# The decay differences of a chunked linear attention, issued on VectorE instead of GpSimd

## The reference

```python
def chunked_gated_linear_attention(q, k, v, log_g):
    '''S_t = diag(g_t) S_{t-1} + k_t^T v_t ; o_t = q_t S_t, evaluated chunkwise.'''
    ...
# ab_layer: GLA_HEADS = 4, key size 128, value size 256
ob = chunked_gated_linear_attention((qb * GLA_DK ** -0.5), kb, vb, log_a)
# cd_layer: HGRN_HEADS = 8, key and value size 128
od = chunked_gated_linear_attention(silu(qd), 1.0 - f, idd, log(f))
```

## Time and profile before

| | |
|---|---|
| median of 3 runs | 3214.06 us (3213.27 to 3218.4) |
| the profiled execution | 3213.27 us, of which the profile's span is 3212.0 us |
| TensorE busy | 3055.3 us (95%) |
| VectorE busy | 2129.2 us (66%) |
| ScalarE busy | 1527.7 us (48%) |
| GpSimd busy | 164.7 us (5%) |

### The profile page before, as it was taken

How to read it: one execution, slowest core, us unless ns; L and a number is a source line. 1 busy time by engine, 2 the same in 40 slices (tenths; PEclk the granted TensorE clock), 3 DMA queues, 4 the chain that set the end, 5 groups by cost and what they waited for, 6 DMA issues and landing times. The chain is left out here.

```text
span 3212.0 us, 57240 instructions
## 1 busy us (share of the span) xinstructions
PE 3055.3 (95%) x25845; PEld 2600.1 (81%) x25870; DVE 2129.2 (66%) x2024; ACT 1527.7 (48%) x1406; POOL 164.7 (5%) x292
## 2 busy tenths in 40 slices
PE   8999899999999999999999999998999899789896
PEld 7888788888888787587888888887686787657785
DVE  5555766666556666458687786555665547898785
ACT  4343654445434544745555555334554534333652
POOL 0000000000000000001200000000400000002220
PEclk9999999999999999999999999999999999899998
DMA  8665456655656454445766666563545445554331
GB/s 287 208 205 191 139 203 210 209 197 195 225 185 210 149 172 167 169 158 166 260 236 213 228 230 216 205 202 115 171 157 188 167 171 186 171 184 168 119 135 62
DMA packets 295477, 596.75 MB, mean 186 GB/s; under 512 B 11825, under 2 KB 16049, under 8 KB 295105
## 3 DMA queue, kind: packets, MB, share of 16 engines
q1 hardware_dynamic: 287616, 564.22, 51.4%
q0 software_dynamic: 7616, 28.87, 2.4%
HBM read 577.32 MB, written 15.73 MB: 185 GB/s over the span
## 5 line engine op out<-in xcount | busy, mean ns | idle before, releaser
L1489 DVE TENSOR_TENSOR WL<-WF,WH 128x2048 bf16<-128x2048 f32 x533 | 1208.5, 2288 | 682.3 <-ACT WH L999 682.1
L531 PE MATMUL PSG<-XH,WH 128*128 128x256 bf16 x5648 | 1549.9, 274 | 52.4 <-DVE XL L1594 26.3
L531 PE MATMUL PSG<-XL,WH 128*128 128x256 bf16 x5648 | 1549.7, 274 | 0.0
L531 PE MATMUL PSG<-XH,WL 128*128 128x256 bf16 x5648 | 1548.8, 274 | 0.0
L999 ACT ACTIVATE WH<-WF 128x2048 bf16<-128x2048 f32 x533 | 999.9, 1899 | 615.4 <-PE PSG L531 372.2
L531 PE MATMUL PSG<-SCR,WH 128*128 128x256 bf16 x4480 | 736.8, 273 | 0.0
L531 PEld LDWEIGHTS PSG<-XH,WH 128*128 128x128 bf16 x5648 | 556.4, 99 | 134.7 <-issue 65.5
L531 PEld LDWEIGHTS PSG<-XL,WH 128*128 128x128 bf16 x5648 | 555.9, 98 | 69.9 <-issue 1.2
L531 PEld LDWEIGHTS PSG<-XH,WL 128*128 128x128 bf16 x5648 | 556.1, 98 | 67.8
L531 PE MATMUL PSG<-SCR,WL 128*128 128x256 bf16 x2240 | 610.6, 273 | 0.0
L531 PEld LDWEIGHTS PSG<-SCR,WH 128*128 128x128 bf16 x4480 | 438.5, 98 | 55.0
(11 more groups left out here) (240 smaller groups left out, 1652.5 us busy)
## 6 DMA issues: line engine op xcount, KB each, us to landing
WF<-ffn_w_up SPq DMA_DIRECT2D x176, 1024.0 KB, 5.8
WF<-ffn_w_down SPq DMA_DIRECT2D x88, 1024.0 KB, 5.1
WF<-ab_w_in SPq DMA_DIRECT2D x56, 1024.0 KB, 5.2
WF<-a_w_in SPq DMA_DIRECT2D x48, 1024.0 KB, 6.0
WF<-cd_w_in SPq DMA_DIRECT2D x48, 1024.0 KB, 5.2
WF<-a_w_out SPq DMA_DIRECT2D x16, 1024.0 KB, 5.1
WF<-kv_w_k SPq DMA_DIRECT2D x16, 1024.0 KB, 5.1
WF<-b_w_q SPq DMA_DIRECT2D x16, 1024.0 KB, 5.1
```

The source lines that it names most:

```text
L531: return nc.tensor.matmul(o, lhsT, rhs, start=start, stop=stop, skip_group_check=True)
L1489: tt(l, w, h, ALU.subtract).then_inc(s_lo, 1)
```

## The change

The 15 instructions per head go from GpSimd's stream to VectorE's. The first 14 are the same operations with the same operands; the last becomes a tensor_scalar with b's column 127 as the pointer operand. decay(0) and decay(1) take the first two side steps of VectorE's flow, ahead of weigh(0), which were empty; decay(h+2) takes step 5 of head h, right after the step with weigh(h+1), which was empty too. ScalarE's and TensorE's streams stay as they are. GpSimd has no compute left in these stretches; its DMA issues stay in their order.

```diff
         def gpsimd_program():
-            def decays(P):
-                for h in range(P["H"]):
-                    n, bb, e = P["base"] + h, P["b"][:, h, :], P["E"][h % 2]
-                    if h >= 2:
-                        nc.gpsimd.wait_ge(s_prod, 2 * n - 2)
-                    for l in range(1, 8):
...
-                        nc.gpsimd.tensor_tensor(to[:, :, 0:half], mid, src[:, :, 0:half], ALU.subtract)
-                        nc.gpsimd.tensor_tensor(to[:, :, half:width], src[:, :, half:width], mid, ALU.subtract)
-                    last = bb[:, 127:128].broadcast_to([128, 128])
-                    nc.gpsimd.tensor_tensor(e[:, 7, 0:128], last, bb[:, 0:128], ALU.subtract).then_inc(s_dec, 1)
...
-            nc.gpsimd.wait_ge(s_scan, 1)
-            decays(GLA)
...
-            nc.gpsimd.wait_ge(s_scan, 2)
-            nc.gpsimd.wait_ge(s_xs, 16)
-            nc.gpsimd.wait_ge(s_yb, 16)
-            decays(HGRN)
...
             def gla_heads(P):
+                def decay(h):
+                    n, bb, e = base + h, P["b"][:, h, :], E[h % 2]
+                    if h >= 2:
+                        nc.vector.wait_ge(s_prod, 2 * n - 2)
+                    for l in range(1, 8):
+                        width = 2 ** l
+                        half = width // 2
+                        src = bb.rearrange("p (n w) -> p n w", w=width)
+                        to = e[:, l - 1, :].rearrange("p (n w) -> p n w", w=width)
+                        mid = src[:, :, half - 1:half].broadcast_to([128, T // width, half])
+                        tt(to[:, :, 0:half], mid, src[:, :, 0:half], ALU.subtract)
+                        tt(to[:, :, half:width], src[:, :, half:width], mid, ALU.subtract)
+                    ts(e[:, 7, 0:128], bb[:, 0:128], bb[:, 127:128], -1.0, ALU.subtract, ALU.mult).then_inc(s_dec, 1)
...
                     if h + 1 < H:
                         weigh(h + 1)
                     yield
+                    if h + 2 < H:
+                        decay(h + 2)
                     yield
                     yield
                     yield
...
-                yield
+                decay(0)
+                yield
+                decay(1)
                 yield
                 weigh(0)
```

## The result

The changed kernel takes 3240.1 us (median of 4 runs, 3235.8 to 3245.9) against 3214.2 us before (4 runs, 3213.3 to 3218.4). The ratio is 1.0075, its 95% interval 1.0055 to 1.0095. The forecast was 3239 us. The profiled execution of the changed kernel took 3238.2 us with a span of 3236.9 us. That is 24.9 us more span than before (3212.0).

The account below looks back on a forecast made before the run. TensorE, busy 95% of the span, bounds GLA; HGRN has about 30 us of TensorE holes. GLA 8.6 + HGRN 18 = 26.6 us, taken as 26 on 3213.3, gives 3239 us; own range 3233 to 3246, wider range 3222 to 3252.

Parts of the forecast that it names:

- The rates: VectorE: decay 0.207 us an instruction, 3.1 us a head; 37 us of work added, 13 regained from weigh, net 24.
- GLA, forecast 8.6: GLA stretch: 4.4 + 1.5 + 1.1 + 1.6 = 8.6 us, all staying because TensorE is full there.
- The start: GLA start: TensorE stands 4.4 us as decay(0) delays weigh(0), then 1.5 us more at the lower clock.
- the steps after it: GLA heads 0 and 1: later exponentials delay TensorE's norm by 1.1 us, then 1.6 more in the next head.
- HGRN, forecast 18: HGRN stretch: delays at the start and heads 0 to 5, 18 us; heads 6 and 7 have no decay.
- forecast step: HGRN norms: start +0.3, head 0 +2.4, then +6.3, +2.0, +3.1, +1.0 and +2.9 us for heads 1 to 5.
- not only work, it is also queued: VectorE: decay also waits behind mask, sum, scaling, weigh and often a split, so ScalarE waits longer at exponentials.
- Throughput alone: Rival: only net VectorE work on the chain counts, 11 us in HGRN, 4.4 at GLA's start; 3229 us, 27%.
- No change: Rival: VectorE's slack and the lead of three chunks cover each shift, TensorE sees nothing; 3213 us, 6%.
- Stalls that slow the clock: Rival: each of six longer TensorE waits brings 1.5 us more at the lower clock; 3248 us and up, 12%.
- Faster: Rival: decay falls in VectorE's idle time and six HGRN heads give back 7.5 us; 3206 us, 7%.
- VectorE's idle time ahead of the split: GLA start: 8.69 us idle ahead of 2298.33 cannot be used, since the wait for the split stands ahead of decay.

Follow-up runs that it names:

- e8: e6 plus 11 spare VectorE reductions, which nothing reads, at each place where the change has decay(h+2); 3225.1 us, ratio 1.0033.
- e6: Against the kernel before: decay(0) and decay(1) of both layers hoisted into VectorE's idle time, the other decays on GpSimd; 3213.0 us, ratio 0.9992.
- e5: Changed kernel with decay(0) and decay(1) hoisted into VectorE's idle time and decay(h+2) issued ahead of weigh(h+1); 3220.5 us, ratio 1.0017.
- e4: Changed kernel with decay(0) and decay(1) hoisted: behind the scan for GLA, behind the last S5 update for HGRN; 3225.3 us, ratio 1.0034.
- e11: e9 with eight chained GpSimd memsets in place of four, so Exp starts later with no added VectorE instruction; 3248.2 us, ratio 1.0107.
- e9: e6 with GpSimd's decays of heads 2 and up replaced by four chained memsets, leaving those decays out; 3217.8 us, ratio 1.0012.
- e10: e9 plus the 11 spare VectorE reductions at each place where the change has decay(h+2); 3219.9 us, ratio 1.0019.
- e3: Changed kernel with decay(h+2) issued ahead of weigh(h+1) in the same step, same instructions; 3231.0 us, ratio 1.0052.

## Why the prediction was right

**The rates held.** Decay was forecast at 0.207 us an instruction and 3.1 a head. It is 0.202 us and, from its start at 2303.86 to that of the next decay at 2306.89, 3.03. VectorE's net was to rise by 24 us and rose by 22.2. Weigh is at 285 ns in all twelve heads, 3.32 us a set.

**GLA, forecast 8.6, measured 10.0.** The start was right to the tenth: a wait of 4.42 us (4.4) and a product set that is 1.49 us longer (1.5). By the starts of the head norms, less the 3.3 us by which this execution was late at the scan, the stretch was 6.8 us late at head 0 (2339.31 against 2329.21) and 8.1 at head 1 (2362.37 against 2350.98). By TensorE's rows the start was 6.1 of this, so the steps after it were 0.7 and 1.3 us (forecast 1.1 and 1.6). The last 1.9 us came behind them, where I had nothing: TensorE waits for the mask in front of the next product, and that product runs at the lower clock.

```profile
2364.69 3.50 PE L506 MATMUL PB<-SCR 128*128 128x128 f32 x16 [1.22 <-DVE SCR L1903]
```

Before, it came without a wait and took 1.95 us. Some 1 us of the loss came back where an old stall of 0.80 us vanished.

**HGRN, forecast 18, measured 13.5.** Against the last S5 update, which starts 11.4 us later than before, TensorE's landmarks stand like this:

| head norm, start in us | h0 | h1 | h2 | h3 | h4 | h5 | last chunk (L2003) | end |
|---|---|---|---|---|---|---|---|---|
| before | 2998.05 | 3018.74 | 3048.18 | 3074.20 | 3095.60 | 3114.26 | 3146.26 | 3212.0 |
| after | 3010.21 | 3036.93 | 3068.17 | 3097.08 | 3119.70 | 3140.78 | 3173.39 | 3236.9 |
| late by, less 11.4 | 0.8 | 6.8 | 8.6 | 11.5 | 12.7 | 15.1 | 15.7 | 13.5 |
| step | 0.8 | 6.0 | 1.8 | 2.9 | 1.2 | 2.4 | 0.6 | -2.2 |
| forecast step | 2.7 | 6.3 | 2.0 | 3.1 | 1.0 | 2.9 | 0 | 0 |

From head 1 to head 5 every step held to 0.5 us, the large one of 6 us with its reason: decay(3) behind weigh and a split, Exp at 3028.61, L1274 at 3036.49. At head 4 the number held by luck. I had put a late mask or a late L1274 there, but between the norms of heads 3 and 4 TensorE waits for neither any longer than before. The 72 matmuls of a chunk take 8.9 us instead of 7.9, at a granted clock of 0.88 where it was 1.00, behind head 3's wait of 4.12 us (0.53 before). The term that was mis-sized is the first. I had put +0.3 at the start and +2.4 at head 0, and my own times for that norm (3000.5 against 2998.05) hold the 0.3 already, so the sum counted it twice. In fact TensorE waits 1.42 us for weigh(0) at 2983.69, which I had not seen, but the 2.93 us it used to wait for the mask in front of the next product shrink to 1.16, and that product takes 2.02 us at the full clock instead of 3.56. The delay swallowed another stall and its slow clock. So head 1's norm is 6.8 us late, where the prediction named some 9. The second miss is the end: the same work behind the last chunk took 2.2 us less, because the granted clock was 0.81 and 0.89 over it. In the kernel before:

```profile
3146.00:3156.00 10.00, 9.74 (x67) 7.71 (x68) 6.97 (x5) 6.42 (x4) 0.00 (x0) 0.73 0.22 71
...
3170.00:3212.00 42.00, 26.13 (x211) 21.93 (x208) 17.90 (x23) 4.93 (x5) 0.00 (x0) 0.85 0.15 51
```

So 3239 against 3240.1 is closer than the working deserves. The two stretches were forecast at 26.6 us and cost 23.5 in the profile, and the interval of the ratio alone is 6 us to either side.

**The mechanism.** The forecast said that decay on VectorE is "not only work, it is also queued". In GLA lateness is shown to be all of it. Extra VectorE work that nobody waits for left the stretch as it was (e8: 146.3 as in e6), and the hoist and the order gave back 8.1 of 10.0, and 1.7 of the rest are the hoist's own cost (e5). e4 has the changed kernel's exponentials of heads 2 and 3, 3.4 and 6.3 us later behind the mask than e6, and is 2.4 us over e6. That e11 costs 10.0 us over e9, as much as the change, is chance: the change loses 6.1 of its 10.0 at the start, which e11 leaves alone, and in e11 the two exponentials are 5.5 and 7.5 us later than in e6.

In HGRN both count. Position gave back 10.6 of 13.5 us (e5), and a later Exp alone can cost 19.9 (e11, with more delay than the change has). But spare work costs 3.3 to 10.5 us there (e10, e8), by the products and exponentials that stand behind it and that ScalarE or TensorE wait for. The two costs do not add up: where Exp is late anyway, work on VectorE fills time in which it would have idled. e5, whose Exp starts 0.5 to 2.1 us later behind the mask than in e6, is 6.6 us over e6 in HGRN. TensorE waits 3.0 us for weigh there, which now stands behind decay and for which it does not wait in e6, and 2.1 us longer for L1274; it is 1.6 us longer busy with the same instructions. How the 13.5 us of the changed kernel itself divide between the two costs stays open.

**The rivals.** *Throughput alone* (3229 us) falls as the whole cause: it gave GLA only its start and HGRN 11 us, and reordering the same work moved the time by 7 to 9 us (e3). Its 11 us for HGRN are near what e8's spare work costs (10.5), but there too a wait for what stands behind the work is what TensorE sees. *No change* falls by TensorE's 15.6 us of new waits for L1274. *Stalls that slow the clock* was half there. In GLA TensorE's same instructions were busy for 146.5 us instead of 143.2, so the lower clock cost 3.3 us where 1.5 were forecast. In HGRN it cost 1.1 at head 4 and 0.5 at the norm of head 1 (1.19 instead of 0.67 us behind its wait of 5.88), and gave 1.5 and 2.2 us back elsewhere: 217.7 us against 218.9 in all. *Faster* needed decays that end ahead of GpSimd's. Even e5, the best order found with all decays on VectorE, is 0.17% slower than before. The Trainium skill's advice to put elementwise work on VectorE ("GPSIMD Engine Reference", section "4.1 Engine selection") is borne out in the rate (0.202 against 0.40 us) but not in the time: the place in the queue decided.

**What the prediction got wrong in the reasoning.** That VectorE's idle time ahead of the split could not be used for the first decays was true for the place that the change gave them, not for the engine: behind the scan there was room, at the price of one TensorE wait of 1.56 us (e4, e6).

## What to carry to other kernels

Before moving work to a faster engine, write down what stands ahead of it in that engine's queue and when its result is then ready. Here the work ran twice as fast and its exponentials came 2 to 6 us later, and a third engine passed the delay on to TensorE. A step that feeds an in-order engine belongs ahead of work that can wait, and the first steps of a flow belong as far ahead as their inputs allow, though either move delays what it passes (here weigh, and one split). To learn what lateness costs, delay the result on an idle engine, by as much as the change does and no more. And do not add two such prices: delays that run side by side cost as much as the longer one.

## What the runs showed of the hardware

- A GpSimd instruction with two SBUF inputs is held while VectorE runs such instructions back to back, not only for one of them: 4.36 us for one that takes 0.40 alone, through the rest of weigh's sixteen and the split behind them (e9). The Trainium skill ("SBUF — State Buffer", section "Who interferes with whom") says that a VectorE instruction with two SBUF inputs contends with a GpSimd instruction that reads SBUF and not with one that only writes it. The runs agree with both halves: beside GpSimd's memsets weigh stays at 286 ns an instruction, beside its subtractions it takes 328 to 338 in the mean.
- VectorE starts independent 128-column instructions every 0.20 us although each lasts 0.28 us (decay in the changed kernel, from 2303.86 us on).
- Lateness is not linear here. From the mask of half 1 to the start of Exp for the head after next it is 6 to 9 us in e6 (17.5 at one head), 7 to 12.5 in e9 (16.2 at one) and 12 to 16 in e11. The first step, up to 3.6 us, cost 4.8 us of time, with weigh faster at the same time; the second, 2.6 to 6.4 us at seven of eight heads, cost 30.4, of which 12.2 us are TensorE's same instructions at a lower granted clock.
- A stall can pay for itself in part. Where the change delayed TensorE ahead of an old wait, that wait shrank from 2.93 to 1.16 us and the product behind it ran in 2.02 instead of 3.56 us.
